# Experts of a mixture layer sorted by token count and multiplied in pairs of 128 and 64 slots, with eight weight chunks of a pair taken whole in float32

## The reference

```python
logits = (xt @ router_w).astype(jnp.float32)
top_logit, top_idx = lax.top_k(logits, TOP_K)          # TOP_K = 2, N_EXPERTS = 8
gates = jax.nn.softmax(top_logit, axis=-1)
...
def swiglu(x, w1, w2):                                  # w1: 1024 x 5632, w2: 2816 x 1024
    gate, up = jnp.split(x @ w1, 2, axis=-1)
    return (jax.nn.silu(gate) * up) @ w2
...
yb = yb * slot_gate[:, None].astype(yb.dtype)
y = jnp.zeros_like(xt).at[slot_tok].add(yb)
```

## Time and profile before

| | us |
|---|---|
| median of 3 runs | 1502.48 |
| lowest of the runs | 1501.88 |
| highest of the runs | 5215.01 |
| span of the profiled execution | 1499.8 |
| TensorE with a matmul in flight, share of the span | 98% |

### The profile page before, as it was taken

How to read it: one execution, slowest core, us unless ns; L and a number is a source line. 1 busy time by engine, 2 the same in 40 slices (tenths; PEclk the granted TensorE clock), 3 DMA queues, 4 the chain that set the end, 5 groups by cost and what they waited for, 6 DMA issues and landing times.

```text
span 1499.8 us, 21512 instructions
## 1 busy us (share of the span) xinstructions
PE 1470.4 (98%) x8395; PEld 1278.7 (85%) x8395; DVE 1172.5 (78%) x1150; ACT 944.0 (63%) x963; POOL 52.2 (3%) x58
## 2 busy tenths in 40 slices
PE   7999999999999999998999999999999999999997
PEld 7989898999889989897788888888888888888885
DVE  7878655555447878655998988989989899898996
ACT  6655444444437654444777778777787777777774
POOL 0031000000000131000000000000000000000000
PEclk9999999999999999999999999999999999999999
DMA  8443443445546433534799989999999999999994
GB/s 311 141 141 113 168 164 117 169 171 195 181 164 219 141 113 117 193 114 167 282 359 382 347 341 364 352 378 361 340 357 347 380 362 343 361 347 377 365 357 157
DMA packets 54478, 388.41 MB, mean 259 GB/s; under 512 B 6000, under 2 KB 6256, under 8 KB 8176
## 3 DMA queue, kind: packets, MB, share of 16 engines
q1 hardware_dynamic: 53840, 384.98, 68.7%
q10 hardware_dynamic: 544, 2.10, 0.4%
HBM read 386.00 MB, written 1.05 MB: 258 GB/s over the span
## 4 chain that ended last, share of the span: by engine, by line
PE 92%; DVE 3%; DMA 2%; ACT 1%; issue 1%; POOL 0%; SPq 0%; DVEq 0%; ACTq 0%
PE pb L1059 27%; PE pb L1061 27%; PE pb L1060 27%; PE pb L1461 1%; PE pb L1424 1%; PE pb L1207 1%; PE pb L1289 1%; PE pb L1309 1%; DVE xTl L1636 1%; DMA arena<-in_mem 1%; DVE wlo L2177 1%; PE pb L1040 1%; PE pb L1447 0%; PE pb L1448 0%; DMA raw<-in_lin_w 0%
## 5 line engine op out<-in xcount | busy, mean ns | idle before, releaser
L2177 DVE TENSOR_TENSOR wlo<-raw,whi 128x2048 fp32r<-128x2048 f32 x175 | 400.3, 2291 | 47.7 <-ACT whi L961 46.2
L961 ACT ACTIVATE whi<-raw 128x2048 fp32r<-128x2048 f32 x175 | 335.6, 1920 | 131.9 <-PE pb L1061 131.9
L1587 DVE TENSOR_TENSOR wlo<-raw,whi 128x2048 fp32r<-128x2048 f32 (+1 forms) x101 | 226.0, 2246 | 133.2 <-ACT whi L602 133.0
L1059 PE MATMUL pb<-whi,mTh 128*128 128x512 f32 x768 | 305.2, 397 | 1.6 <-DVE wlo L2177 1.6
L1061 PE MATMUL pb<-whi,mTl 128*128 128x512 f32 x768 | 300.1, 391 | 0.0
L602 ACT ACTIVATE whi<-raw 128x2048 fp32r<-128x2048 f32 (+1 forms) x101 | 189.9, 1884 | 172.3 <-PE pb L1061 167.3
L1059 PE MATMUL pb<-xTh,whi 128*128 128x256 f32 x736 | 210.2, 286 | 2.7 <-DVE xTl L1624 1.2
L2177 DVE TENSOR_TENSOR kvXr<-kvX,whi 128x2048 fp32r<-128x2048 f32 x86 | 196.7, 2291 | 19.3 <-ACT whi L961 17.7
L1060 PE MATMUL pb<-xTl,whi 128*128 128x256 f32 x736 | 208.2, 283 | 0.0
L1061 PE MATMUL pb<-xTh,wlo 128*128 128x256 f32 x736 | 208.2, 283 | 0.0
L1060 PE MATMUL pb<-wlo,mTh 128*128 128x512 f32 x528 | 205.6, 389 | 0.0
(11 more groups left out here) (341 smaller groups left out, 2195.4 us busy)
## 6 DMA issues: line engine op xcount, KB each, us to landing
raw<-in_ffn_w SPq DMA_DIRECT2D x209, 1024.0 KB, 4.8
kvX<-in_ffn_w SPq DMA_DIRECT2D x88, 1024.0 KB, 4.9
raw<-in_lin_w SPq DMA_DIRECT2D x64, 1024.0 KB, 4.8
raw<-in_lin_w SPq DMA_DIRECT2D x4, 536.0 KB, 5.6
arena<-in_mem ACTq DMA_DIRECT2D x2, 1024.0 KB, 8.5
h<-in_x SPq DMA_DIRECT2D x1, 1024.0 KB, 4.9
out<-xn SPq DMA_DIRECT2D x2, 512.0 KB, 3.1
consts<-in_con SPq DMA_DIRECT2D x1, 838.0 KB, 13.6
```

The costliest lines, as they stand in the source:

```text
L961: nc.scalar.activation(whi[:, (MOE0 + c) % HRING, :], xraw_slots[c % XRING], ACT.Copy).then_inc(hi_ready, 1)
L1059: nc.tensor.matmul(o, lh, rh, start=first, stop=False)
L1587: V.tensor_tensor(wlo[:, m % RING, c], raw[:, m % RING, c], whi[:, m % HRING, c].bitcast(F32), ALU.subtract).then_inc(lo_ready, 1)
L2177: V.tensor_tensor(xlo_slots[c % XRING], xraw_slots[c % XRING], whi[:, (MOE0 + c) % HRING, :].bitcast(F32), ALU.subtract).then_inc(lo_ready, 1)
```

## The change

**Pairs.** The experts are sorted by their token counts on the chip (VectorE's max and max_index over count x 8 + expert number, on seven experts; expert 0 keeps its place at the head). Expert 0 and the three fullest others are "H" with 128 slots; the four emptiest are "L" with 64 slots (`LIGHT`). H number i and L number i are worked on together, L three turns behind H. A turn (`turns()`) is one unit of H and one of L; a unit is a group of w1 (two chunks) or one chunk of w2, 22 units an expert. SyncE reads the sorted numbers into registers (L607) to find the chunks. The second pass now also runs if the fourth fullest of the seven has more than 64 tokens, or expert 0 more than 128.

**Light experts.** The 64 high columns and 64 low columns of an L expert's tokens lie side by side as one 128-column operand. Each depth tile takes two matmuls instead of three, one with the chunk's high part and one with its low part; rows 0 to 63 of the result belong to the high tokens, rows 64 to 127 to the low ones. ScalarE copies the lower rows (`low_rows`), VectorE adds them to the upper (`lsum`, 64 x 512), then come silu (`lsilu`), product (`lgated`), transposes of 64 columns (`turn_light`) and the split into `xhL`. In w2 the two halves of the output rows are summed by the spreading, whose selection holds the 64 slots twice.

**Whole chunks.** In groups 0, 1, 2, 4, 5, 6, 8 and 9 of an H expert (`WHOLE`) the second chunk of w1 isn't split. It is multiplied as it landed, in float32, with an unsplit copy of the tokens (`xgf`): four matmuls of 512 columns instead of twelve. TensorE waits for its landing itself, and it takes no `whi` buffer.

**The rest.** The ring of chunks has seven slots (`XRING`), the seventh in the arena. The gate is no longer applied when h is added to (L2154), but as the scale of the output evacuation (`gs`, made by small float32 matmuls in `turn_selections`). Both experts of a pair are spread and added together, once a pair instead of once an expert. The gather makes 192 columns a depth tile instead of 256; the first one is split into 128 for H and, one turn later, 64 for L. The loops over pairs are unrolled on every engine.

```diff
-XRING = 6
+XRING = 7
...
+LAG = 3
+LIGHT = P // 2
+WHOLE = (0, 1, 2, 4, 5, 6, 8, 9)
...
+def turns():
+
+    total = PAIRS_E * UNITS
+    return [((divmod(a, UNITS) if a < total else None), (divmod(a - LAG, UNITS) if a >= LAG else None))
+            for a in range(total + LAG)]
...
+STREAM = [(kind, at[0], c) for step in turns() for kind, at in zip("HL", step) if at
+          for c in unit_chunks(at[1])]
+SPLIT = [n for n, (kind, _, c) in enumerate(STREAM) if not whole(kind, c)]
...
             def load_experts(p):
...
+                for n, (kind, i, c) in enumerate(STREAM):
+                    at = p * NSTREAM + n
+                    if at >= XRING:
+                        sp.wait_ge(w_used, MOE0 + at - XRING + 1)
...
+                        q = column(kind, i)
+                        ids[kind, i] = sp.value_load(eid[0:1, q:q + 1].bitcast(U32), min_val=0, max_val=NE - 1)
+                    e = ids.get((kind, i), 0)
+                    slot = landed(p, n)[0]
+                    sp.dma_start(xraw_slots[slot], ffn_w[1 + e, c]).then_inc(x_loaded[slot], 16)
```

The turn as ScalarE's queue has it, and VectorE's sum of the light rows behind its splits:

```diff
+                for a, (full, light) in enumerate(turns()):
+                    if full:
+                        i, u = full
+                        splits_through(SIDX["H", i, unit_chunks(u)[-1]])
...
+                    if behind:
+                        light_silu(*behind)
...
+                        if u < NF // 2:
+                            act.wait_ge(w_used, unit_end(p, "H", i, u))
+                            nc.scalar.activation(xsilu[:, u % 2, :], pb[:, u % 2, 0:S], ACT.Silu).then_inc(silu_ready, 1)
...
+                    if light:
+                        i, u = light
+                        splits_through(SIDX["L", i, unit_chunks(u)[-1]])
+                        if u < NF // 2:
+                            act.wait_ge(w_used, unit_end(p, "L", i, u))
+                            nc.scalar.activation(low_rows[0:LIGHT, :], pb[LIGHT:P, 3 + u % 2, :], ACT.Copy).then_inc(low_ready, 1)
...
+                            dve.wait_ge(low_ready, pair_no(p, i, u))
+                            V.tensor_tensor(lsum[0:LIGHT, :], low_rows[0:LIGHT, :], pb[0:LIGHT, 3 + u % 2, :],
+                                            ALU.add).then_inc(lsum_ready, 1)
```

TensorE's products, the wait ahead of the light transposes, and the addition to h:

```diff
+                            if kind == "L":
+                                both = xg[:, k, P:2 * P]
+                                nc.tensor.matmul(o, both, w[0][:, kk, :], start=first, stop=False)
+                                mm = nc.tensor.matmul(o, both, w[1][:, kk, :], start=False, stop=last)
+                            elif len(w) == 1:
+                                mm = nc.tensor.matmul(o, xgf[:, kk, :], w[0][:, kk, :], start=first, stop=last)
+                            else:
+                                mm = split_product(o, [xgh[:, k, 0:P], xgHl[:, k, :]],
+                                                   [part[:, kk, :] for part in w], first, last)
...
+                def turn_light(i, j):
+
+                    pe.wait_ge(lg_ready, pair_no(p, i, j))
...
-                        ins = V.scalar_tensor_tensor(out=hh, in0=pb[:, 6 + half, :],
-                                                     scalar=gates[:, t, bass.ds(col, 1)], in1=hh,
-                                                     op0=ALU.mult, op1=ALU.add)
+                        ins = V.tensor_tensor(hh, hh, pb[:, b, :], ALU.add)
```

More of the change, by code:

```diff
@@ L284, in build @@
+        xlo_slots = [kvXr[:, 0, :], kvXr[:, 1, :]] + [wlo[:, (MOE0 + i) % RING, :] for i in range(RING)] + [
+            over("raw6r", RAW6, CW)]
         raw12 = small_(NT * 12).rearrange("p (t c) -> p t c", c=12)
@@ L983, in experts, with splits_through @@
-                for phase in range(2):
-                    gathered_hi(p * (NE // 2), phase, 6 - 2 * phase)
-                act.wait_ge(routed_ok, 1)
-                with act.Fori(0, NE // 2 - 1) as pair:
-                    two_experts(pair, False)
-                two_experts(NE // 2 - 1, True)
+                w = par_("ffn_w", 1)
+                done = [HRING]
+                def splits_through(n):
+                    while done[0] < NSPLIT and SPLIT[done[0] - HRING] <= n:
+                        split_high(p, done[0])
+                        done[0] += 1
@@ new lines, in spread_half @@
+                def spread_half(half):
+                    pe.wait_ge(last_lo, 2 * p + half + 1)
+                    c = slice(half * 512, (half + 1) * 512)
+                    for t in range(NT):
+                        turned_to = selT[:, 1, t * P:(t + 1) * P]
+                        nc.tensor.matmul(last_bank(half, t), turned_to, yLh[:, c], start=False, stop=False)
+                        nc.tensor.matmul(last_bank(half, t), turned_to, yLl[:, c], start=False,
+                                         stop=True).then_inc(last_spread, 1)
```

788 lines of the change are left out of this document (493 added, 295 removed).

## The result

| | us |
|---|---|
| before, median of 4 runs | 1502.18 |
| after, median of 4 runs | 1473.1 (1471.73 to 1478.61) |
| ratio | 0.982, 95% interval 0.980 to 0.984 |
| span of the profiled execution after | 1471.6 |
| forecast | 1460, range 1438 to 1502 |

The kernel is 1.8% faster. The direction and the range hold; the time lies 13 us above the forecast, inside the band of 2%, to which the prediction gave a chance of 0.33, against 0.58 for a larger gain.

What follows compares the result with a forecast made beforehand. Loads were to take over from TensorE: first slot freed 718.0, 257 chunks 701.6, latency 2.1, start 4, ordering 12, tail 19.8 us give a span of 1457.5; runs lie 2.7 above: 1460 us, range 1438 to 1502.

Steps and rivals of the forecast that it cites:

- TensorE's prices: Expert part: split chunk 2.72 us, whole chunk 3.46, light chunk 1.81, gather matmul of 256 columns 0.124.
- the case of 0.32: Gather: F32R matmuls of 192 columns take four times their columns, 0.32 us each; three pairs' gathers cost 19 us more.
- VectorE and ScalarE: Expert part: both get less work, VectorE 159 us a pair instead of 168, ScalarE 139.
- The loads take over: Expert part: loads need 180 us a pair at 384 GB/s, TensorE 168, so most of TensorE's 91 us isn't gained.
- The ordering term: Expert part: uneven turns cost the loads 3 us a pair, 12 in all, beside 4 at the start.
- The layout by hand: Kinds of turns priced against their loads: several at the loads' pace, none far above; 2.3 us wait in one light group of eleven.
- Both in w2: 4.53 against 5.46: Eight turns a pair with H and L in w2: 4.53 us against loads of 5.46.
- Last landing to the end of its split: Tail: 4.3 us from the last chunk's landing until its split is done, then 15.5 to the span's end.
- Rival 1: Light groups: product, copy, sum, silu and transposes stand behind splits and aren't hidden; 1492 us, chance 19%.
- Rival 2: Expert part: loads were already at their ceiling, 356 GB/s or 2.95 us a chunk; 1504 us, chance 10%.
- Rival 3: Expert part: TensorE's clock halves after waits for loads; 1573 us at a quarter of its work, chance 6%.
- Rival 4: Second pass runs if one token more exceeds the limit of 64, repeating all 264 chunks; 2181 us, chance 2%.

Runs made afterwards that it cites:

- The deferral: Light transposes and the split behind them moved behind the next turn's H unit, against the kernel after: 1448.23 us, ratio 0.9654 to the kernel before.

## Why the prediction was right, and what was 13 us off

By its own steps.

**TensorE's prices hold, its sum not quite.** A whole chunk 3.43 us (3.46 forecast). Narrow matmuls in F32R take 0.11 us, whether of 64, 128 or 192 columns, against 0.124 for 256: they hardly gain below 256 columns, which is the forecast's first case, and the case of 0.32 falls. But TensorE's busy time is 687 us from 716 to 1440 and 19 from there to the end, 706 against 671 forecast: 176 us a pair instead of 168, close to the 180 of the loads. Some 10 us of it are matmuls at the lower clock level (an estimate from their count); the rest lies in small restarts, as in the turn from 763.76 to 774.31 us, which takes 10.55 us with a matmul always in flight instead of 10.1.

**VectorE and ScalarE hold.** 612.5 and 523.6 us busy over 716 to 1440 and at most 21 and 15 behind it, by four 158 and 135 a pair (159 and 139 forecast).

**"The loads take over" holds in part, with a wrong rate.** ScalarE waits for loads, issue to landing rises from 4.8 to 7.1 us, and taking a slot away costs some 7 to 12 us. But a kernel bound by loads alone wouldn't gain from less work on TensorE, and with a third of the products it gains 61 us: TensorE, at 0.95 of its time, still holds the loads back. The 384 GB/s taken as the ceiling were read off windows in which SyncE still waited for TensorE: at the share 0.96 there are 374 GB/s, by which full share would be 390, and 408 with most of TensorE's products left out. At 408, 257 chunks take 660 us, not 702. If the loads can have that rate beside all products, which no run shows, the ceiling was 41 us too pessimistic and hid an error on the other side; that the forecast came within 13 us is then in part luck.

**The ordering term failed.** The forecast put 16 us into start and order. Measured in its own frame: the first slot is freed at 715.6 (718.0); the last chunk lands at about 1446.5, where the DMA engines run dry, so 257 chunks take 730.9 us instead of 701.6 + 2.1 + 4 + 12 = 719.7; from there to the span's end 25.1 (19.8). -2.4 + 11.2 + 5.3 = +14.1, which is 1471.6 against 1457.5; the median lies 1.5 us above the span, not 2.7. The -2.4 isn't only the shorter gather: the kernel before had a granted clock of 0.57 over 709 to 713 us, the kernel after 1.00. Three places make up the rest.

- *The end of L's w1.* The layout by hand had waits of 0.75 us in the turns with four splits, where the trace has 0.80 to 0.86, and one of 2.3 us where H enters w2, where it has 1.99. What it lacks are the waits of the turns behind, 1.10, 1.10 and 2.89 us: five waits of together 7.9 us from 822 us on. For the turns with H in w2 and L in w1 its sums are right (8.0 against 8.2 us; VectorE's turns are 8.0 us apart) and the loads stay at 0.98. The step that fails is the row "Both in w2: 4.53 against 5.46". The first of these turns still has the last light product and its transposes, and too little of L's work to cover them. TensorE's 2.89 us there hold up ScalarE, VectorE and SyncE in turn, and the loads lose about 15 us in four pairs, half of what the share of 0.96 lacks. The deferral, which takes these waits away, gives 24.9 us; of these the clock is some 3.
- *The start.* Share 0.70 over 26 us against 0.96 later is 7 us, 4 were put in; 1 to 2 us of it are the dip of the clock there.
- *The tail.* "Last landing to the end of its split" was put at 4.3 us and took 9.0. The last part, 16.1 us, was forecast at 15.5.

The end of the stream, on which the 9.0 rests, in the loads' share and rate (40 slices of 1430 to 1460 us, 0.75 us each), ScalarE and VectorE:

```profile
DMA  9999999999999998999996110000000000000000
```

```profile
1447.88 1.92 ACT L782 ACTIVATE whi<-raw 128x2048 fp32r<-128x2048 f32 x1 [1.43 <-PE pb L1203]
1449.71 1.09 ACT L1118 ACTIVATE yHh<-pb,route 128x1024 fp32r<-128x1024 f32 x1
1450.70 1.90 ACT L782 ACTIVATE whi<-raw 128x2048 fp32r<-128x2048 f32 x1
...
1453.24 2.28 DVE L1883 TENSOR_TENSOR wlo<-raw,whi 128x2048 fp32r<-128x2048 f32 x1
```

The chunk is there at about 1446.5, and ScalarE comes to it at 1450.70, after the split before it, which waited for TensorE, and after H's output (1.09 us). The forecast took a free engine.

**Rival 1** (the light path's chain isn't hidden, 1492 us) had the mechanism. TensorE waits at L1708 as it said, though not in every group: 34.2 us in 24 of 44, 0.8 us a group, below its point of decision of 1.1. So the forecast's case gave the time to within 1%, and rival 1's mechanism its miss; the two weren't exclusive, and should have been one forecast with a term between them. **Rival 2** falls: 374 GB/s in this kernel, 408 with less on TensorE. The Trainium skill's figure of about 358 GB/s ("DMA: Bandwidth & Descriptors", Specifications) is no ceiling here. The Trainium skill's page "Perfetto Trace Analysis", section Roofline, says that a core alone may take more than that share, up to some 435 GB/s of its DMA engines. The 408 and 423 measured agree. **Rival 3** was there in small: the lower clock level for some 3 to 5 us once a pair, behind the longest wait in three pairs and behind the 1.96 us wait in the second; some 3 us of the kernel's time in all. **Rival 4** didn't occur: the fourth fullest of the seven has its 64 tokens, and the chunks were loaded once.

What was to show it: a DMA share of 0.97 or more was missed (0.96 over 742 to 1440, at 374 GB/s), TensorE at most 0.95 busy in the expert part holds (660.77 of 698), and the last chunk landed inside the window of 1410 to 1450.

What stays open: why the start runs at a share of at most 0.76 in every version, why TensorE's clock falls there in some executions and not in others, whether TensorE or the loads hold the deferred version's pace, and how much of the step from 387 to 408 GB/s could be had with all products in place.

## What to carry to other kernels

When work is taken off the engine that sets the pace, check the next resource not only by its sum per stage but by the order inside each queue: a short instruction behind a long one, waited for by the relieved engine, can stop the new bottleneck through the buffers it holds. The cheap remedy was to let the waiting engine do its next independent unit first, and not to move the producer, which only put the stop into another queue. A load rate read while something else sets the pace is a lower bound for the ceiling, even where the DMA engines look busy all the time. And before a few us are put down to an edit, look whether the two profiled executions differ ahead of the place that it touches.

## What was not expected of the hardware

- With a third of TensorE's products the loads of this core reach 408 GB/s over 638 us and 423 over 80, where the kernel before had 382 in the windows of the earlier trace rows, at a share of 0.98 to 1.01 in both. The time from issue to landing grows from 4.8 to 7 and 9 us with it.
- A product of 64 x 256 float32 values takes GpSimd 2863 ns, seven times VectorE's 410, while VectorE's splits run beside it; those of 128 x 256 ahead of the expert part took 679 and 1382 ns, by line.
- The same wait isn't always followed by the same clock. Behind the four waits of 2.89 to 2.91 us all twelve matmuls ran at the lower level (0.427 us apart) in two pairs, nine of them, from the third on, in one, and none in one; of the waits of 1.99, 1.96 and 1.98 us in the same turn of three pairs only that of 1.96 was followed by the lower level.
- F32R matmuls of 64, 128 and 192 columns all start 0.11 us apart, of 256 columns 0.124, of 512 0.227.
- A float32 matmul of 512 columns takes 0.857 us, 3.8 times the F32R one of 0.227, a little under four.
